# Layer 2's expert loop: three of four blocks as pairs of experts, weights placed by matrix kind and block parity

## The reference, cut to what matters

```python
N_EXPERTS, TOP_K, EXPERT_FF, D_MODEL = 64, 8, 256, 1024
scores = sigmoid(h @ router_w)                       # 256 x 64
top_e  = top_k(scores + bias within the best 4 of 8 groups, 8)
gate   = scores[top_e] / sum * 2.5
# for every expert e, on the tokens routed to it:
hb = silu(xb @ w1[e]) * (xb @ w3[e])                 # 1024 -> 256
acc[tok] += (hb @ w2[e]) * gate                      # 256 -> 1024
```

## Time and profile before

| | us |
|---|---|
| median of 3 runs | 2621.48 (2621.4 to 2625.0) |
| profiled execution: span from first to last instruction | 2617.6 |
| median less that span: what lies around it | 3.9 |
| layer 2's loop, from its first expert transfer to its last products | 2018.3 to 2586.7 |
| PE busy over the span | 2484.3 (95%) |
| TensorE's granted clock over the span | 0.989 |

### The profile page before, as it was taken

How to read it: one execution, slowest core, us unless ns; L and a number is a source line. 1 busy time by engine, 2 the same in 40 slices (tenths; PEclk the granted TensorE clock), 3 DMA queues, 4 the chain that set the end, 5 groups by cost and what they waited for, 6 DMA issues and landing times.

```text
span 2617.6 us, 36012 instructions
## 1 busy us (share of the span) xinstructions
PE 2484.3 (95%) x12508; PEld 1680.1 (64%) x12508; DVE 982.1 (38%) x2221; ACT 525.7 (20%) x1167; POOL 233.6 (9%) x377
## 2 busy tenths in 40 slices
PE   7999999999999999999999799999998999999997
PEld 4878888888875455455545368778885544444443
DVE  1436624548167211111111286545717311111115
ACT  2234511325131111111111213234511000000000
POOL 0000000000000122111112000000000121111110
PEclk9999999999999999999999999999998999999999
DMA  9874445445365999999999674774453999999995
GB/s 329 266 231 142 146 135 166 146 148 173 129 231 208 379 420 409 418 414 394 413 415 398 266 260 147 243 238 153 145 172 112 366 412 396 401 394 395 388 383 235
DMA packets 293667, 733.84 MB, mean 280 GB/s; under 512 B 33366, under 2 KB 208606, under 8 KB 238352
## 3 DMA queue, kind: packets, MB, share of 16 engines
q1 hardware_dynamic: 267120, 681.78, 69.4%
q0 software_dynamic: 26400, 50.07, 5.0%
HBM read 725.62 MB, written 51.54 MB: 297 GB/s over the span
## 4 chain that ended last, share of the span: by engine, by line
PE 69%; DMA 25%; DVE 4%; SPq 1%; issue 1%; ACT 0%; DVEq 0%; ACTq 0%; POOLq 0%
DMA arena<-in_w 23%; PE psum L890 16%; PE psum L1175 14%; PE psum L1102 6%; PE psum L901 5%; PE psum L1317 3%; PE psum L916 3%; PE psum L1187 3%; PE psum L1137 2%; PE psum L1133 2%; PE psum L1355 2%; PE psum L771 1%; PE psum L753 1%; PE psum L1084 1%; PE psum L832 1%; DMA arena<-in_w_in 1%
## 5 line engine op out<-in xcount | busy, mean ns | idle before, releaser
L890 PE MATMUL psum<-arena 128*128 128x256 f32 x1984 | 445.6, 381 | 1.8 <-DMA arena<-in_w_in 1.0
L1175 PE MATMUL psum<-arena 128*128 128x512 f32 x832 | 381.1, 602 | 35.3 <-DMA arena<-in_w 35.3
L890 PEld LDWEIGHTS psum<-arena 128*128 128x128 f32 x1984 | 372.2, 190 | 60.7 <-issue 5.8
L1317 PE MATMUL psum<-arena 128*64 128x256 f32 (+1 forms) x2848 | 337.7, 382 | 21.7 <-DMA arena<-in_w 19.7
L1317 PEld LDWEIGHTS psum<-arena 128*64 128x64 f32 (+1 forms) x2848 | 213.4, 139 | 118.1 <-DMA arena<-in_w 15.8
L1175 PEld LDWEIGHTS psum<-arena 128*128 128x128 f32 x832 | 152.2, 193 | 197.7 <-issue 154.8
L1187 PE MATMUL psum<-arena 128*128 128x512 f32 x440 | 206.3, 612 | 5.9 <-DVE arena L2200 3.2
L1940 DVE SCALAR_TENSOR_TENSOR grow<-psum,par,grow 128x255 f32<-128x255 f32 (+1 forms) x304 | 136.1, 479 | 125.8 <-ACT grow L1531 120.2
L1102 PE MATMUL psum<-arena 128*128 128x256 f32 x768 | 173.2, 379 | 0.0
L2576 POOL DMA_INDIRECT results<-arena,ids x90 | 92.9, 1032 | 861.2 <-DVE arena L2474 469.9
L2474 DVE COPY arena<-psum 128x512 f32<-128x512 f32 x50 | 34.6, 691 | 342.3 <-PE psum L1187 195.3
(11 more groups left out here) (337 smaller groups left out, 2686.8 us busy)
## 6 DMA issues: line engine op xcount, KB each, us to landing
arena<-in_w SPq DMA_DIRECT2D x405, 1024.0 KB, 16.9
arena<-in_w_in SPq DMA_DIRECT2D x92, 1024.0 KB, 5.3
arena<-in_w_ada SPq DMA_DIRECT2D x32, 1024.0 KB, 7.9
arena<-results SPq DMA_DIRECT2D x24, 1024.0 KB, 9.9
arena<-in_w_br_ssm SPq DMA_DIRECT2D x24, 768.0 KB, 4.4
arena<-in_w_ada SPq DMA_DIRECT2D x8, 2048.0 KB, 14.9
arena<-cumulated SPq DMA_DIRECT2D x36, 384.0 KB, 4.2
arena<-in_w_br_four SPq DMA_DIRECT2D x12, 1024.0 KB, 5.2
```

The costliest lines, as they stand in the source:

```text
L890: last = mm(o[:, a, :], w[:, k, a * P:(a + 1) * P], rhs[:, k, :], start=k == 0, stop=k == ks - 1, skip_group_check=True)
L1175: last = mm(o.rearrange("p (a n) -> p a n", a=2), lhs(k), w[:, k, :, :], start=k == 0, stop=k == KD - 1)
L1317: last = mm(bank[0][c, a * FF:(a + 1) * FF], xTe[0][:, k, c], w13[b][:, k, a, :], start=k == 0, stop=k == KD - 1)
```

## The change

In layer 2 the loop's step now depends on its parity: a step with an even number has two pairs, a step with an odd number a pair and a single. So of four blocks three are pairs, and two steps hold seven experts where they held six. The planner's constants say so (`C_LOAD` = 2*pairs + singles before the step), the loop is unrolled to 24 steps at most instead of 28. With 63 experts, 7 of them over 64 tokens, this gives 18 steps (36 blocks: 27 pairs, 9 singles) where there were 21 (42 blocks: 21 pairs, 21 singles).

The buffers are placed by matrix kind and by the block's parity: w1 and w3 of a block with index 0 in units 0 to 3, of a block with index 1 in units 5 to 8 (two for each kind, a single uses one), and w2 of *every* block in the same two units (`downw`). A single's products go through the same helper as a pair's (`part_products`), w1 and w3 apart. The results' read-back no longer waits for the last `down`, since its targets hold only w1 and w3.

DVE's work ahead of the loop grows: `mark_last` has ten small operations where it had three, `plan_steps` three more. GpSimd reads the last two blocks' columns from a table. Layer 1 keeps its loop.

```diff
-ROUNDS = {0: -(-STEPS // 8), 1: 28 // 2}
+ROUNDS = {0: -(-STEPS // 8), 1: 24 // 2}
+LAST_PAIRS, LAST_SINGLES = 36, 12
...
+def mixed_before(step):
+    return 2 * step - step // 2, step // 2
...
+        pack[:, C_LOAD + STEPS + step] = 2 * pairs + singles
...
+        up_at = [[[0, UNIT], [2 * UNIT, 3 * UNIT]], [[5 * UNIT, 6 * UNIT], [7 * UNIT, 8 * UNIT]]]
+        upw = [[[arena[:, o:o + UNIT] for o in part] for part in parts] for parts in up_at]
+        downw = [arena[:, o:o + UNIT] for o in (4 * UNIT, u2T_at + UNIT)]
...
+                def pair_of(at):
+                    return [row_expert(at), row_expert(at + LAST_PAIRS)]
+                def single_of(at):
+                    return [row_expert(at + 2 * LAST_PAIRS)]
+                def block_w1_in(experts, b):
+                    for which, ex in enumerate(experts):
+                        sp.dma_start(upw[b][0][which], matrix("w1", ex)).then_inc(last_w1[b], 16)
+                def block_w3_in(experts, b):
+                    for which, ex in enumerate(experts):
+                        sp.dma_start(upw[b][1][which], matrix("w3", ex)).then_inc(last_w3[b], 16)
+                def block_w2_in(experts):
+                    for which, ex in enumerate(experts):
+                        sp.dma_start(downw[which], matrix("w2", ex)).then_inc(last_w2, 16)
+                def last_layer_loads():
+                    front, back = pair_of(0), pair_of(1)
+                    block_w1_in(front, 0)
+                    block_w3_in(front, 0)
+                    sp.wait_ge(s["shared_up"], of(l, "shared_up", nt))
+                    block_w1_in(back, 1)
+                    sp.wait_ge(e[l]["down"], 3)
+                    block_w3_in(back, 1)
+                    block_w2_in(front)
+                    with sp.Fori(0, ROUNDS[l]) as ii:
+                        def step(u):
+                            i = ii * unr + u
+                            with sp.If(n > i):
+                                with sp.If(n > i + 1):
+                                    front = pair_of(ii * 3 + mixed_before(u + 1)[0])
+                                    sp.wait_ge(e_half[l], ii * (2 * unr) + (2 * u + 1))
+                                    block_w1_in(front, 0)
+                                    sp.wait_ge(e[l]["up"], ii * (2 * unr) + (2 * u + 3))
+                                    block_w3_in(front, 0)
+                                back = single_of(ii) if u else pair_of(ii * 3 + 1)
                                 sp.wait_ge(e[l]["down"], ii * (2 * unr) + (2 * u + 4))
...
+                                block_w2_in(back)
+                                with sp.If(n > i + 1):
+                                    back = pair_of(ii * 3 + (mixed_before(u + 1)[0] + 1)) if u else single_of(ii)
+                                    sp.wait_ge(e_half[l], ii * (2 * unr) + (2 * u + 2))
+                                    block_w1_in(back, 1)
+                                    sp.wait_ge(e[l]["up"], ii * (2 * unr) + (2 * u + 4))
+                                    block_w3_in(back, 1)
+                                    front = pair_of(ii * 3 + mixed_before(u + 1)[0])
+                                    sp.wait_ge(e[l]["down"], ii * (2 * unr) + (2 * u + 5))
+                                    block_w2_in(front)
+                                if u + 1 < unr:
+                                    step(u + 1)
+                        step(0)
...
-                    for q in ((0, 1, 3, 2) if l and i == 0 else range(TOPK // 2)):
-                        if l:
-                            if (i, q) == (0, 2):
-                                sp.wait_ge(e[l]["down"], sp.snap(n * 2 + 2))
-                            if (i, q) == (1, 1):
-                                sp.wait_ge(e[l]["up"], sp.snap(n * 2 + 2))
-                            if (i, q) == (1, 3):
-                                sp.wait_ge(e[l]["down"], sp.snap(n * 2 + 3))
+                    if l and i == 1:
+                        sp.wait_ge(e[l]["up"], sp.snap(n * 2 + 2))
+                    for q in range(TOPK // 2):
...
+                def part_products(b, a, experts):
+                    for k in range(KD):
+                        for which in range(experts):
+                            c = slice(which * HALF, (which + 1) * HALF) if experts == 2 else slice(0, P)
+                            w = upw[b][a][which].rearrange("p (k n) -> p k n", k=KD)
+                            last = mm(bank[b][c, a * FF:(a + 1) * FF], xTe[b][:, k, c], w[:, k, :], start=k == 0, stop=k == KD - 1)
+                    return last
+                def block_up(i, b, experts, loads, between):
+                    pe.wait_ge(z["xt_act"], i + 2)
+                    pe.wait_ge(z["xt_dve"], i + 2)
+                    pe.wait_ge(z["h_ready"], i + 1)
+                    pe.wait_ge(last_w1[b], loads)
+                    part_products(b, 0, experts).then_inc(e_half[l], 1)
+                    between()
+                    pe.wait_ge(last_w3[b], loads)
+                    part_products(b, 1, experts).then_inc(z["up"], 1)
+                def block_down(i, b, experts, loads):
+                    down_ready(i)
+                    pe.wait_ge(last_w2, loads)
+                    weights = [w.rearrange("p (k n) -> p k n", k=2) for w in downw]
+                    (two_downs(hT[b], weights) if experts == 2 else down(hT[b], weights[0])).then_inc(z["down"], 1)
...
+                def last_layer_blocks():
+                    x_transpose(0, 0, 1)
+                    block_up(0, 0, 2, 32, lambda: x_transpose(1, 1, 1))
+                    with pe.Fori(0, ROUNDS[l]) as ii:
+                        def step(u):
+                            i = ii * unr + u
+                            g = lambda k: ii * (2 * unr) + (2 * u + k)
+                            back = 1 if u else 2
+                            with pe.If(n > i):
+                                with pe.If(n > i + 1):
+                                    x_transpose(g(2), 0, ii * unr + (u + 2))
+                                block_up(g(1), 1, back, ii * 48 + (48 if u else 32), lambda: block_ht(g(0), 0))
+                                block_down(g(0), 0, 2, ii * 112 + (96 if u else 32))
+                                with pe.If(n > i + 1):
+                                    x_transpose(g(3), 1, ii * unr + (u + 2))
+                                    block_up(g(2), 0, 2, ii * 64 + 32 * (u + 2), lambda: block_ht(g(1), 1))
+                                    block_down(g(1), 1, back, ii * 112 + (112 if u else 64))
+                                with pe.If(n < i + 2):
+                                    block_ht(g(1), 1)
+                                    block_down(g(1), 1, back, ii * 112 + (112 if u else 64))
+                                if u + 1 < unr:
+                                    step(u + 1)
+                        step(0)
...
-                    link(V.tensor_scalar(sloti[0][:, n8, :], sloti[1][:, n8, :], PAIRS_AT - 1, None, ALU.bitwise_and))
-                    link(V.tensor_copy(before_last[:, n8, :], sloti[0][:, n8, :]))
-                    link(V.tensor_scalar(before_last[:, n8, :], before_last[:, n8, :], 1.0, steps, ALU.add, ALU.is_lt))
+                    link(V.tensor_scalar(far_by, singles, 2.0, float(PAIRS_AT), ALU.mult, ALU.add))
+                    link(V.scalar_tensor_tensor(last_from, steps, -1.0, singles, ALU.add, ALU.subtract))
+                    link(V.tensor_scalar(before_last[:, n8, :], slotc[:, n8, :], float(PAIRS_AT), far_by, ALU.is_ge, ALU.mult))
+                    link(V.tensor_tensor(before_last[:, n8, :], slotc[:, n8, :], before_last[:, n8, :], ALU.subtract))
+                    link(V.tensor_scalar(before_last[:, n8, :], before_last[:, n8, :], last_from, None, ALU.is_lt))
+                    link(V.scalar_tensor_tensor(last_pair, steps, float(LAST_SINGLES - 1), singles, ALU.add, ALU.add))
+                    link(V.scalar_tensor_tensor(odd_one, singles, -2.0, steps, ALU.mult, ALU.add))
+                    link(V.scalar_tensor_tensor(last_back, last_pair, 1.0, last_from, ALU.add, ALU.subtract))
+                    link(V.scalar_tensor_tensor(last_back, last_back, odd_one, last_from, ALU.mult, ALU.add))
+                    link(V.tensor_copy(bexp[0:1, P + 1:P + 3], plan[0:1, 20:22]))
```

More of the change, by code:

```diff
@@ L90, in host_constants @@
     pack[:, C_FOLD:C_FOLD + HALF] = (p[:, None] % HALF) == np.arange(HALF)
[L91 to L102 removed]
+    for row in range(3 * STEPS):
+        which, step = row // STEPS, row % STEPS
+        alone = which == 2 or (which == 0 and lone(0, step))
+        far = which == 0 and alone
+        place = step - pairs_before(0, step) if far else step if alone else pairs_before(0, step)
+        pack[row, C_ROW:C_ROW + 5] = (place, not alone, which == 1, alone, far)
+    for row in range(2 * LAST_PAIRS + LAST_SINGLES):
+        which = row // LAST_PAIRS
```

(28 more changed lines are left out.)

222 lines of the change are left out of this document (114 added, 108 removed).

## The result

| kernel | median of the runs, us | ratio to before, 95% interval | profiled span, us |
|---|---|---|---|
| before | 2623.22 | 1 | 2617.6 |
| after | 2635.26 | 1.0043 [1.0032, 1.0054] | 2633.4 |

The account below looks back on a forecast made before the run. The prediction took the second layer's expert loop to run at the pace of its transfers, set by the slowest DMA engines. Terms -8.5 + 1.8 + 0.9 + 0 + 0.5 = -5.3 us took 2621.5 to 2616 us, range 2600 to 2632.

Parts of the forecast that it names:

- PE's work 0: Second layer's expert loop: six blocks fewer save 72 us of PE work, none on the path, worth 0.
- matrices 0: Second layer's expert loop: 18 steps still load 63 experts, 189 matrices as before, worth 0.
- Rows by engine, -8.5 (bounds 0, -10.8): Gathers and scatters in the loop: the busiest DMA engines carry fewer rows, -8.5 us.
- -1.5 us at the last pair: Behind the loop: last pair's down ends 9.4 us after the last single's w3 lands, not 10.9, -1.5 us.
- Rows do not matter: Rival on the loop's transfers: engines are slow for another reason, transfers take what they took; 2624.7 us, chance 0.19.
- the slow engines serve the upper rows: Rival on the loop's gathers and scatters: the slow engines' load grows, +8.5 us; 2633 us, chance 0.05.
- One w2 buffer, +1.8: Loads held until each down ends: queue empty only after the first two downs, +1.8 us, bounds 0 and +13.5.
- dry queue: Rival: transfer queue runs dry before each of nine singles, 1.5 us each, 13.5 in place of 1.8; 2628, chance 0.18.
- PE waits longer, clock stays at 1.00: Pair blocks in the loop: 5.3 us idle in pieces of at most 2.1 us, clock stays 1.00, worth 0.
- a falling clock: Sign in the loop: the prediction would be wrong if the clock fell there; no size given.
- Ahead of the loop +0.9: Before the loop: added DVE operations take 2.2 us, next loads go at 2043.0 instead of 2042.10, +0.9 us.
- behind it +0.5: After the loop: -1.5 us at the pair's down, +1.5 for the last single's w2, +0.5 for the results' read-back.

Follow-up runs that it names:

- e9: e5 with layer 2's single-expert ranks spread over all 128 partitions, three more VectorE operations in the planner; 2596.79 us, ratio 0.9905 to the kernel before.
- e12: Kernel before with e4's rank order and layer 2's singles over all 128 partitions, the marks' table kept intact; 2594.35 us, ratio 0.9891.
- e5: Kernel after with both e2's own w2 buffers and layer 2's ranks 0 to 7 standing 4 partitions apart; 2604.17 us, ratio 0.9929 to before.
- e2: Kernel after with separate w2 buffers for each block parity, w2 asked for one down earlier; 2614.66 us, ratio 0.9971 to before.
- e4: Kernel before with layer 2's ranks 0 to 7 standing 4 partitions apart in a block's 64 partitions; 2609.19 us, ratio 0.9952.
- e7: Kernel before with every odd rank in a half of layer 2 swapped with its mirror (quad e with quad 7-e); 2604.88 us, ratio 0.9937.
- e1: Kernel after with two filler matmuls on TensorE before the w2 wait of both downs of even steps; 2631.5 us, ratio 1.0040 to before.
- e8: e2 with e1's two filler matmuls ahead of the even steps' down products; 2613.83 us, ratio 0.9970 to the kernel before.
- e6: Kernel after with SyncE's store of the gates issued ahead of its last-step wait for the pair's down; 2633.6 us, ratio 1.0044 to before.

## Why the prediction was wrong

*PE's work 0, matrices 0: right.* 189 matrices, and 72 us of products less that bring nothing. e9 and e12 show it most plainly: 36 blocks or 42, evenly loaded, 2596.8 and 2594.4 us.

*Rows by engine, -8.5 (bounds 0, -10.8): right in sign and mechanism, a little small.* The table has the rows of the busiest engine, counted from the routing by the rule of the Trainium skill ("DMA: Bandwidth & Descriptors", "The descriptor swizzle"). Beside them stands the time by which the median is less (e5 and e9 against e2, the others against the kernel before), and the stretch from the first load of the flow to the start of the last down in each profiled execution (the earlier trace rows for the kernel before, 2042.10 to 2581.31). The last column is the mean rate of the transfers from 2110 to 2510 us:

| kernel | busiest engine, rows | us less | us a row | stretch, us | GB/s |
|---|---|---|---|---|---|
| before | 496 | | | 539.2 | 396 |
| e4 | 412 | 12.6 | 0.15 | 526.9 | 405 |
| e7 | 386 | 17.6 | 0.16 | 523.6 | 407 |
| e12 | 314 | 27.8 (+0.6 of planner) | 0.16 | 512.3 | 418 |
| e2 (after, own w2) | 426 | | | 528.5 | 405 |
| e5 | 364 | 10.5 | 0.17 | 519.1 | 411 |
| e9 | 316 | 17.9 (+0.6) | 0.17 | 513.0 | 418 |

By that rule these runs agree, to a few us over 182 rows. The stretches do so for both kernels alike: against the 539.2 us before, each of the six is 0.14 to 0.15 us shorter for every row fewer, and the rate of the transfers never falls as the rows of the busiest engine do. No view names an engine, so the rule is borne out by these times alone. The change takes the busiest from 496 to 426: 70 x 0.15 or 0.16 = -10.5 to -11.2 us, and the stretch of e2, the change without the shared buffer, is 10.8 us shorter than before. The pace of the downs shows less of it: two steps take 60.3 us in e2, where the prediction had 59.4 if rows count and 60.6 if not. So the two ends of the stretch, the forecast's -1.5 us at the last pair among them, have a part in the 10.8 that no run separates; the rate, 405 GB/s where it was 396, is the firmer sign that the rows count between the two kernels too. The working took halves, not engines (1.33 of the mean, when 496 is 1.94 of the 256); that the two came out alike was luck. A row's price stood in the earlier trace rows: 16 x 44.8 us over 4096 rows are 0.175 us. "Rows do not matter" and "the slow engines serve the upper rows" fall with it.

*One w2 buffer, +1.8: this is the step that failed.* It said that for a single "it is 5.8 - 3.65 = 2.1 us", and that this "just covers" the 1.7 us from an issue to flowing data. Each of its three parts was off. The 5.8 took a matrix at the loop's mean 2.89 us, though with a pure stream it is 2.5 (the earlier trace rows had 2.49), and took the down to start as w2's last byte lands; but the two matrices behind it were through some 2.7 us after that start (2204.30 to about 2207), so TensorE starts about 5.0 - 2.7 = 2.3 us behind the data. The 3.65 became 5.33, at a granted clock of 0.50 behind a wait of 2.98 us. The 1.7 us from issue to a full share is nearer 3 (issue at 2209.83, share 0.93 in the 2 us from 2213). So not +0.4 us of margin but a hole of 3.8 us; e1, at full clock, still has one of 3. What it costs is shown by e2: 4.9 us at the start, where the prediction had its 1.8, then 2.0 us in each two steps, 13.9 in seven of them, and 2.1 up to the last down, 20.9 in all, with 2.8 behind it. The rival "dry queue" had the place and the sign, and with 1.5 us a single too small a price, 2628; even the upper bound, 13.5 us, was below what was measured.

*PE waits longer, clock stays at 1.00: wrong.* Waits of up to 3.7 us came, and stretches at 0.5 (the lower of the two levels, 1.2 GHz) behind them. The prediction had named a falling clock as a sign of being wrong. Its price is small all the same: e8 shows none with a full queue, and with a dry one e1 gains 3.8 us by the medians and 4.7 in the stretch.

*Ahead of the loop +0.9, behind it +0.5:* the first is borne out to about a microsecond. The loads start at 2044.57 against 2042.10 in the earlier trace rows, 2.5 us later, and VectorE's first operation on the router's scores is 0.95 us late already (2000.03 against 1999.08), so the added operations make 1.5 us. The second was short by what the shared buffer does: the last w2 arrives so late that the down waits 2.96 us, and gates and results stand behind it. From the start of the last down to the end of the span it is 39.5 us, where it was 36.3 before and is 36.7 in e2; e6 shows that moving the gates alone does not help.

Put together, in the profiled executions: the loads start 2.5 us later, the stretch is 549.3 us instead of 539.2 (-10.8 by everything but the shared buffer, rows and ends together, and +20.9 by the shared buffer), and the end takes 3.2 us more, 15.8 us in all. The forecast without its +1.8 was 2614.4, and e2 measured 2614.66. That they meet to 0.3 us is luck: e2's profiled execution, its median, was 4.3 us behind the one before (1993.47 against 1989.17) ahead of anything that the change touches, and by the other runs' price the rows are worth 2 to 3 us more than was forecast.

## What to carry to other kernels

When a load may only be issued once a product has ended, ask what the queue still holds when that product starts. Its margin is that much transfer time less the product's duration and less the time from issue to flowing data. The product starts some time behind its own last byte, and during this time the queue already works off what it holds; and it may run at the lower granted clock. Where a unit of work gets smaller (a single), the margin is to be worked out for the smallest. A DMA-bound loop is paced by its busiest engine: count the partial transfers' rows by engine, and spread them before shortening anything else. Here that spreading is worth 28 us with an edit to a table of constants and three small operations, on the kernel before as it stands (e12, 2594.35 us, better than both kernels), against 12 us lost by the change.

## What the runs showed of the hardware

- Where a row of 4 KB lies among the 128 partitions of a gather or scatter decides what it costs: 0.15 to 0.17 us for each row fewer in the busiest of 16 engines, counted by the rule named above, from 496 down to 314, with no sign of flattening.
- The transfers of one core ran at 415 to 420 GB/s in all four stretches of 100 us from 2110 to 2510 us once the rows were nearly even (e9), where the kernel before had 389 to 406.
- A wait of 2.98 us by TensorE was followed by a stretch at a granted clock of 0.50 in the kernel after; with two filler products in it and at most 1.86 us of wait left (e1), every down of a pair in the loop took 3.65 us. Not every long wait does it: in e2 the down at 2123.6, after 3.47 us, took 3.65 us too.
- That TensorE starts about 2.3 us behind the last byte is worked out from shares and bytes, and was not measured by itself.
